# Adding matmuls with unread results to the recurrent stage of a hybrid-decoder step

## The reference

```
d = where(causal, a[..., :, None] - a[..., None, :] + li[..., None, :], -inf)
m_t = maximum(inter, max(d, axis=-1))
w = exp(d - m_t[..., None]) * einsum('bthk,bshk->bhts', q, k)
num = einsum('bhts,bshv->bthv', w, v) + einsum('bht,bthk,bhkv->bthv', e_inter, q, C)
den = sum(w, axis=-1) + e_inter * einsum('bthk,bhk->bht', q, n)
h = num / maximum(abs(den), exp(-m_t))
```

## Time and profile before

| | us |
|---|---|
| three timed runs | 2008.69, 2012.48, 2011.48 |
| their median | 2011.48 |
| the profiled execution's own time | 2009.03 |
| its span in the trace | 2007.4 |
| recurrent stage, from the first L501 to the start of L535 | 179.18 to 253.47 |

### The profile page before, as it was taken

One profiled execution on the slowest core, in us unless ns is written; L12 is line 12 of the kernel. 1 busy time (PEld: TensorE's weight loads), 2 busy tenths in 40 slices (PEclk: granted clock), 3 DMA queues, 4 the chain that ended last, 5 costly groups with the idle time before them and its releaser, 6 DMA issues.

```text
span 2007.4 us, 23398 instructions
## 1 busy us (share of the span) xinstructions
PE 1830.7 (91%) x8410; PEld 1404.4 (70%) x8410; DVE 1213.2 (60%) x1250; ACT 925.8 (46%) x808; POOL 92.0 (5%) x155
## 2 busy tenths in 40 slices
PE   5999979999979878888799999999999999999994
PEld 4746657999954553347587787877878778787783
DVE  2102684444344332223488888888888888888886
ACT  1100022443211111102477777777777677777774
POOL 2100020001001002200100000000000000000001
PEclk9995559999989568898799999999999999999997
DMA  9910042434724002202399999999999999999993
GB/s 275 366 44 1 0 48 89 165 100 130 223 87 171 10 0 62 70 14 105 135 368 370 357 369 338 388 359 359 370 338 386 358 360 369 341 380 353 371 366 138
DMA packets 219023, 458.37 MB, mean 228 GB/s; under 512 B 11189, under 2 KB 45562, under 8 KB 218762
## 3 DMA queue, kind: packets, MB, share of 16 engines
q1 hardware_dynamic: 209034, 428.96, 59.7%
q0 software_dynamic: 8656, 28.13, 5.0%
q10 hardware_dynamic: 1280, 0.54, 0.2%
HBM read 447.11 MB, written 17.30 MB: 231 GB/s over the span
## 4 chain that ended last, share of the span: by engine, by line
PE 83%; DVE 7%; ACT 5%; issue 2%; DMA 2%; POOL 0%; SPq 0%; ACTq 0%; POOLq 0%; DVEq 0%
PE bank L388 15%; PE bank L390 15%; PE bank L389 15%; PE bank L384 8%; ACT wpart L1580 3%; PE wide L390 2%; PE wide L388 2%; PE wide L389 2%; PE bank L759 2%; DVE wpart L916 2%; PE bank L568 2%; PE wide L742 2%; PE bank L800 2%; PE bank L703 1%; PE wide L397 1%
## 5 line engine op out<-in xcount | busy, mean ns | idle before, releaser
L916 DVE TENSOR_TENSOR wpart<-mring,wpart 128x2048 fp32r<-128x2048 f32 x339 | 775.5, 2290 | 159.3 <-ACT wpart L1580 158.4
L1580 ACT ACTIVATE wpart<-mring 128x2048 fp32r<-128x2048 f32 x336 | 643.0, 1917 | 202.3 <-PE bank L390 109.1
L388 PE MATMUL bank<-wpart,xgp 128*128 128x512 f32 x896 | 360.5, 402 | 7.5 <-DVE wpart L916 5.3
L390 PE MATMUL bank<-wpart,xgp 128*128 128x512 f32 x896 | 354.4, 396 | 0.0
L389 PE MATMUL bank<-wpart,xgp 128*128 128x512 f32 x896 | 354.3, 395 | 0.0
L388 PEld LDWEIGHTS bank<-wpart,xgp 128*128 128x128 f32 x896 | 168.5, 188 | 54.4 <-DVE wpart L916 12.9
L390 PEld LDWEIGHTS bank<-wpart,xgp 128*128 128x128 f32 x896 | 168.4, 188 | 41.1
L389 PEld LDWEIGHTS bank<-wpart,xgp 128*128 128x128 f32 x896 | 168.7, 188 | 37.5
L388 PE MATMUL bank<-ffparts,wpart 128*128 128x288 f32 (+1 forms) x528 | 159.3, 302 | 5.4 <-DVE ffparts L916 4.2
L390 PE MATMUL bank<-ffparts,wpart 128*128 128x288 f32 (+1 forms) x528 | 157.4, 298 | 0.0
L389 PE MATMUL bank<-ffparts,wpart 128*128 128x288 f32 (+1 forms) x528 | 155.1, 294 | 0.0
(11 more groups left out here) (344 smaller groups left out, 2150.5 us busy)
## 6 DMA issues: line engine op xcount, KB each, us to landing
mring<-in_w_gate_m SPq DMA_DIRECT2D x114, 1024.0 KB, 5.5
mring<-in_w_up_m SPq DMA_DIRECT2D x113, 1024.0 KB, 5.7
mring<-in_w_down_m SPq DMA_DIRECT2D x112, 1024.0 KB, 5.2
ring<-in_w_in_a SPq DMA_DIRECT2D x6, 2048.0 KB, 24.0
ring<-in_w_down_d SPq DMA_DIRECT2D x8, 1344.0 KB, 7.5
ring<-in_w_gate_d SPq DMA_DIRECT2D x5, 2048.0 KB, 8.7
ring<-in_w_up_d SPq DMA_DIRECT2D x5, 2048.0 KB, 9.0
xrow<-in_zeros POOLq DMA_DIRECT2D x13, 512.0 KB, 13.5
```

Of the source, the lines that this page charges most:

```text
L388: pe.matmul(o, a[0], b[0], start=start, stop=False)
L390: return pe.matmul(o, a[0], b[1], start=False, stop=stop)
L916: return v.tensor_tensor(dst, src, high.bitcast(F32), ALU.subtract)
L1580: a.activation(wpart[:, stage(h), 0, :], mring[:, place(h % IH), :], ACT.Copy).then_inc(S["hi_ready"], 1)
```

## The change

A helper `keep_busy(n)` issues `n` matmuls of the block of ones with the first 256 columns of the constant table, each into `bank[7][:, 0:256]` with `start` and `stop` set. Nothing waits for them and nothing reads what they write. Eight of them stand behind the three waits ahead of the first head, ahead of `scores(0)`. Three stand in each `attend(h)`, behind the matmul that spreads the second row (L509) and ahead of the wait for `W_made`: 8 + 8 x 3 = 32 matmuls in all.

```
+            def keep_busy(n):
+                for _ in range(n):
+                    pe.matmul(bank[7][:, 0:TP], ones, cs[:, 0:TP], start=True, stop=True)
...
             pe.wait_ge(S["gd_free"], n_gd[0])
             pe.wait_ge(S["e_ready"], 1)
             pe.wait_ge(S["inter_ready"], 1)
+            keep_busy(8)
...
                 pe.matmul(bank[4][:, 0:T], ident[0:H, h:h + 1].to_broadcast([H, P]), rA, start=True,
                           stop=True).then_inc(S["m_full"], 1)
+                keep_busy(3)
                 pe.wait_ge(S["W_made"], h + 1)
```

## The result

| | before | changed |
|---|---|---|
| median of 20 runs, us | 2009.77 | 2015.20 |
| the profiled executions' own times, us | 2009.03 | 2015.42 |
| their spans in the trace, us | 2007.4 | 2013.9 |

The changed kernel is slower: the ratio is 1.0027, 95% interval 1.0019 to 1.0034, or 5.4 us. (One run of each, at 3004 and 9450 us, stands far off the others and is out of the comparison.) The forecast had the sign right, inside its range, but its size, +13.9 us, is 2.6 times the measured one.

A forecast was written before the change was run, and what follows sets the result against it. TensorE at half clock was taken to bound the heads. The eight with the first head +0.9, two heads at full clock -2.8, five at half +15.8 gave +13.9 us: 2025 forecast, likeliest case 2016 to 2033, 8-in-10 range 2000 to 2038.

The forecast's parts named there:

- What bounds the stage: In the heads, TensorE at half its clock, busy 49.88 of 50.00 us; VectorE has some 2.7 us to spare a head.
- the added matmuls stand behind the waits: In the stage of the heads, the added matmuls fill no wait worth speaking of and lengthen the path.
- The prices: Three added matmuls in a head cost 3.16 us at half clock; a head at full clock takes 6.9 instead of 8.31.
- The eight and the first head: Ahead of and in the first head: eight cost 5.7 us, raised clock saves 4.8, so it ends 0.9 us later.
- The step that failed: In the later heads, clock holds for the first head and about two more, then mostly stays down: +13.9 us.
- second rival: In the heads, clock falls and rises by turns, n about 5: no change within 4 us, 2008 to 2016; chance 0.12.
- the prompt's attention: Another stage, used as nearest likeness: clock fell once matmuls became groups with waits, then stayed at 0.50 for 78.4 us.
- the forecast's terms: Over the seven later heads, n at full clock: 0.9 - 1.4 n + 3.16 (7 - n) us.
- The sign: Whole kernel: slower, by +13.9 us; chances slower 0.58, same 0.12, faster 0.30.
- Under the first: Rival: clock holds through all heads and into the state product, -11.5 us, or 2000; chance 0.30.
- Under the third: Rival: no rise lasting beyond the eight, n = 0, +23 to +32 us, or 2034 to 2043; chance 0.14.
- The rule of the Trainium skill: For TensorE: clock drops when it pauses too long between bursts, so by it the clock would rise in the eight and hold.

The follow-up runs named there:

- the profile with four: Changed kernel with four added matmuls in each head instead of three, the eight kept: 2018.66 us, 1.0034 against the kernel before.
- the run on thin rows: Changed kernel with the same 32 added matmuls on 32 rows instead of 128: 2036.07 against 2010.10 us before, ratio 1.0125.
- the eight alone: Changed kernel without the three in each head, only the eight ahead of the first scores: 2012.85 us, 1.0012 against the kernel before.
- the three ahead of the wait: Changed kernel with each head's three moved from behind L509 to ahead of the wait for `nd_read`, eight kept: 1996.42 against 2010.10 us before, 0.9948.
- with two: Changed kernel with two added matmuls in each head instead of three, the eight kept: 2026.03 against 2010.08 us before, 1.0082.
- the same product in another order: Kernel before, no added matmuls, samples' carried state multiplied for two heads by turns on 64 rows each: 1994.81 us, 0.9920.
- the best padding: No eight; six added matmuls in the first head, three in each other ahead of the `nd_read` wait: 1997.22 against 2010.08 us before, 0.9932.

## Why the prediction was wrong

- *What bounds the stage, and that the added matmuls stand behind the waits:* right. On the chain of waits the three stand with their whole time at either clock, 2.86 and 1.49 us, and moving them ahead of the wait took 1.14 us from a head. What a head at the full clock would take without them no run shows.
- *The prices:* right at half clock (3.16 predicted for three with two changes of shape; 2.86 plus 0.29 ahead of L520 measured). At the full clock a head takes 7.18, not 6.9 us: from the spread row to the end are 4.69 instead of 4.25, since pieces behind a change of shape shrink by less than half (the first product from 0.56 to 0.33 us, the spread row from 1.25 to 0.75).
- *The eight and the first head:* +5.44 instead of +0.9. The eight took 6.37, not 5.7, and the clock that they had raised fell within 3.4 us, in the scores, so that the first head's three ran at half clock. I had counted the whole first head at the full clock without asking what stands right behind the eight. (Such a head can occur: in the profile with four the clock held through the scores and all of the first head.)
- *The step that failed* is that after a fall the clock "mostly stays down, the three being too short a stream to lift it". Without any eight, the three and the products behind them lift it in the first head, and again in the head after a fall. So in the changed kernel four of the seven heads were at the full clock, not two, and the three others did not cost 3.16 us each but 1.0, 2.0 and 1.4, each being at 1.00 for a part of its time. My own second rival, a fall and rise by turns, had the mechanism, and I gave it 0.12. I let the prompt's attention count for more, whose matmuls stand apart behind waits, while in a head at half clock nothing waits. Its price by the forecast's terms was about 0; with the first head's 5.4 in place of 0.9, and 1.1 in place of 1.4 for a head at the full clock, it would have been 5.4 - 1.1 x 5 + 3.16 x 2 = 6 us, close to the 5.3 of the two profiles. The closeness is in part luck: the profile has four heads at the full clock, not five, and three mixed ones that cost 4.4 us together, where the formula has two at 6.3.
- *The sign* was right by luck in part. The forecast had the loss in the heads behind the first, -2.8 + 15.8 = +13.0 us; they cost -0.1 together. All of the stage's 5.3 us come from the term that it had at 0.9.
- *Two slips in the rivals.* Under the first, full-row streams were said to take a larger share of a head than now; 2.6 of 6.9 and 3.2 of 8.31 are the same 0.38, and the 3.2 counts changes of shape that the 2.6 leaves out. Under the third, the terms as written give 26 and not 23 at the lower end, since they count the first head's three twice; 23 is the forecast's own formula with n = 0.
- *The rule of the Trainium skill* (TensorE: Matmul & The Clock Gate, "Why this matters for your kernels"), that long pauses bring the clock down: the run on thin rows speaks against pauses as the whole cause, with 0.50 under a TensorE that never pauses; and the eight's rise ended without a pause of TensorE.

What stays open: which head falls, and how long a rise lasts. The two later falls of the changed kernel lie inside the three added matmuls, at 217.39 and 251.52 us, right behind a wait that the clock had lasted through in the heads before. Nor does the rise of the eight always end in the scores. In the profiles of the changed kernel, of the eight alone and of the three ahead of the wait it came 5.4 us after the first added matmul and was lost in the second scores, 3.4 us on. In the profiles with two and with four in each head it came 4.5 us after the first added matmul, and lasted through both scores, for 6.8 and 13.65 us. The eight and the scores are the same in all five. What sets the moment of a rise no run here shows, and each kernel was profiled once.

## What to carry to other kernels

Look for the engine's wait at the clock that is aimed at, and put matmuls that fill time ahead of it, not behind it: here that took 1.14 us from a head. What lifted TensorE's clock in these runs was work on full rows without waits between (the prompt's attention, with waits between its groups, stayed at 0.50), and thin work right behind a lift often lost it; two in a head, which lifted it more rarely, cost more than three (16 against 5 us). Before adding work that nobody reads, look for real work that can fill the rows: here the same product in another order gave as much as the best padding (15.3 and 12.9 us, with intervals that overlap), and the two added up.

## What was not expected of the hardware

Matmuls on 32 rows of the array kept TensorE busy for all of the stage without ever raising its clock (0.50 in heads of 10.87 us), where the same matmuls on 128 rows did. Two products of 64 rows each, on different halves of the rows and the same 32 columns, ran side by side: 64 pairs of MATMUL instructions in 9.2 us, 4.1 of them at half clock, against 21.7 us at half clock in the order head by head.
